# Gathered rows cover 256 output features instead of 128 in an expert layer on one core

## The reference, cut to what matters

```python
# z: 256 tokens x 2048, 8 heads, 128 x 128 experts, top 16 of each head
q = z @ peer_wq                               # queries
v1, i1 = top_k(q_first @ keys1, 16); v2, i2 = top_k(q_second @ keys2, 16)
top_s, expert = top_k(v1[i] + v2[j], 16)      # 16 experts of 16384 per head
gate = softmax(top_s)
act  = gelu(peer_u[expert] . z)
out  = sum over 8 heads and 16 picks of gate * act * peer_v[expert]
```

## Time and profile before

| | |
|---|---|
| median of three runs | 3079.88 us |
| the profiled execution, its own time | 3061.2 us |
| its span, first to last instruction | 3059.4 us |
| TensorE matmul busy | 3048.6 us (100%) |
| VectorE busy | 2092.8 us (68%) |
| ScalarE busy | 1562.2 us (51%) |
| GpSimd busy | 1022.9 us (33%) |
| HBM traffic over the span | 213 GB/s |

### The profile page before, as it was taken

The page is one execution under the profiler, slowest core; times in us unless marked ns, Lnnn a source line. Parts: engine busy times, 40 slices in busy tenths (PEclk is TensorE's granted clock), DMA queues, the critical chain, the costliest instruction groups (busy, mean ns, idle before and its releaser), DMA issues.

```text
span 3059.4 us, 42401 instructions
## 1 busy us (share of the span) xinstructions
PE 3048.6 (100%) x16292; PEld 2627.0 (86%) x16292; DVE 2092.8 (68%) x3013; ACT 1562.2 (51%) x2160; POOL 1022.9 (33%) x760
## 2 busy tenths in 40 slices
PE   9999999999999999999999999999999999999999
PEld 7888888888888888888888888888888888888887
DVE  8957985555555666566666789998766855545554
ACT  7654454444554444444444756666566534444443
POOL 0022368888860277666663300000432100000000
PEclk9999999999999999999999999999999999999999
DMA  6557877888876788888886655555555555566664
GB/s 255 172 202 263 319 216 195 240 214 215 213 215 213 255 256 267 264 264 266 268 242 202 193 184 175 173 176 189 188 191 175 190 169 210 188 205 194 194 194 148
DMA packets 388410, 653.91 MB, mean 214 GB/s; under 512 B 65008, under 2 KB 290544, under 8 KB 384752
## 3 DMA queue, kind: packets, MB, share of 16 engines
q1 hardware_dynamic: 306144, 574.70, 58.0%
q10 hardware_dynamic: 37008, 67.88, 6.3%
q0 software_dynamic: 45056, 8.62, 3.7%
HBM read 615.30 MB, written 35.79 MB: 213 GB/s over the span
## 4 chain that ended last, share of the span: by engine, by line
PE 94%; DVE 3%; DMA 1%; ACT 1%; issue 1%; POOL 0%; SPq 0%; ACTq 0%; DVEq 0%; POOLq 0%
PE G L536 40%; PE G L540 20%; PE G L591 4%; PE G L592 4%; PE G L593 4%; PE M L592 3%; PE M L593 3%; PE M L591 3%; PE M L618 2%; PE G L618 2%; PE M L620 2%; PE G L620 2%; PE M L619 2%; PE G L619 2%; DVE lo L1301 1%; DVE CV L1710 1%
## 5 line engine op out<-in xcount | busy, mean ns | idle before, releaser
L1301 DVE TENSOR_TENSOR lo<-raw,hi 128x1024 fp32r<-128x1024 f32 x1088 | 1381.0, 1284 | 567.6 <-ACT hi L918 565.2
L536 PE MATMUL G<-ZA,hi 128*128 128x512 f32 x5098 | 1765.0, 395 | 3.8 <-DVE lo L1301 2.3
L918 ACT ACTIVATE hi<-raw 128x1024 fp32r<-128x1024 f32 x1088 | 1127.4, 1055 | 606.6 <-DMA raw<-in_pv 342.7
L540 PE MATMUL G<-ZA,lo 128*128 128x256 f32 x5114 | 1389.2, 278 | 0.0
L536 PEld LDWEIGHTS G<-ZA,hi 128*128 128x128 f32 x5098 | 943.1, 188 | 210.1 <-DVE lo L1301 2.8
L540 PEld LDWEIGHTS G<-ZA,lo 128*128 128x128 f32 x5114 | 960.8, 188 | 16.6
L2009 POOL DMA_INDIRECT g_scratch<-sel,IDX x256 | 418.4, 1635 | 112.9 <-issue 81.5
L925 ACT ACTIVATE tA<-G 128x256 f32<-128x256 f32 x367 | 139.4, 380 | 578.4 <-PE G L540 577.9
L1307 DVE TENSOR_TENSOR tS<-G,tA 128x256 f32<-128x256 f32 x336 | 141.0, 420 | 326.7 <-ACT tA L925 323.5
L591 PE MATMUL G<-hi,ZB 128*128 128x512 f32 x512 | 199.5, 390 | 0.9 <-DVE lo L1301 0.9
L592 PE MATMUL G<-lo,ZB 128*128 128x512 f32 x512 | 199.2, 389 | 0.0
(11 more groups left out here) (373 smaller groups left out, 2818.6 us busy)
## 6 DMA issues: line engine op xcount, KB each, us to landing
raw<-in_pu SPq DMA_DIRECT2D x256, 512.0 KB, 4.4
raw<-in_pv SPq DMA_DIRECT2D x256, 512.0 KB, 5.2
raw<-in_w_in SPq DMA_DIRECT2D x192, 512.0 KB, 3.5
raw<-in_w_up SPq DMA_DIRECT2D x128, 512.0 KB, 3.5
raw<-in_w_down SPq DMA_DIRECT2D x128, 512.0 KB, 5.0
raw<-in_w_out SPq DMA_DIRECT2D x32, 512.0 KB, 3.5
raw<-in_wq SPq DMA_DIRECT2D x32, 512.0 KB, 4.4
g_scratch<-zero ACTq DMA_DIRECT2D x16, 1024.0 KB, 6.9
```

Of the source, the lines that this page charges most:

```text
L536: pe.matmul(G[:, 0:512], w, Z[:, k, :], start=first, stop=False, skip_group_check=True)
L540: m = pe.matmul(G[:, 0:256], lo[POS[u][p] % NRAW][:, k % 8, :], weights(u, p)[1][:, k, 0:256], start=False, stop=last, skip_group_check=True)
L918: act.activation(hi[w][:, :, :], raw[r][:, :].rearrange("p (k n) -> p k n", k=8), ACT.Copy).then_inc(s_hi, 1)
L1301: dve.tensor_tensor(lo[r][:, :, :], raw[r][:, :].rearrange("p (k n) -> p k n", k=8), hi[w][:, :, :].bitcast(F32), ALU.subtract).then_inc(s ...
```

## The change

- `EDGE` becomes 256: in the last quarter of each chunk the matmuls of the second 128 tokens have 256 columns instead of 384.
- The picked rows cover 256 features. Each pick needs two row DMAs of 128 features and one activation DMA: 384 indirect DMAs in all instead of 256. They come in 16 pieces of 8 picks (16 row DMAs and 8 activation DMAs), 16/5 for each unit. The dots of a piece begin three units after its last pick's unit, and are 256 wide. The ring has three pieces again.
- `load_g` and `load_h` become four DMAs of 512 KB each, two units apart: the gates of chunk c at `VB[c]` - 16, 14, 12, 10, the activations of chunk c at `VB[c-2]` + 8, 10, 12, 14. Each but the first waits until the one before has landed; a gate quarter also waits until GpSimd has used the same quarter of the chunk before. `gate_kept` waits for its own quarter instead of the whole.

```diff
-EDGE = 384
-PIECES = 8
+WIDE = 256
+EDGE = 512 - WIDE
+BLOCK = 8
+PIECES = 128 // BLOCK
+ROWS = WIDE // 128 * BLOCK
+RING = 3
 def picks_by(u):
-    return max(0, min(32 * PIECES, (u - VB[0] + 1) * 9 // 4))
+    return max(0, min((ROWS + BLOCK) * PIECES, (u - VB[0] + 1) * 16 // 5))
 for _b in range(PIECES):
-    _u = min(v for v in range(VB[0], F0) if picks_by(v) >= 32 * _b + 32) + 2
+    _u = min(v for v in range(VB[0], F0) if picks_by(v) >= (ROWS + BLOCK) * (_b + 1)) + 3
     _n = 4 if _b == PIECES - 1 else 2
-    for _k in range(0, 16, _n):
-        DOTS_AT.setdefault(_u + _k // _n, []).extend(range(16 * _b + _k, 16 * _b + _k + _n))
+    for _k in range(0, BLOCK, _n):
+        DOTS_AT.setdefault(_u + _k // _n, []).extend(range(BLOCK * _b + _k, BLOCK * _b + _k + _n))
+def slot_of(b):
+    return (b - PIECES) % RING
...
-                    [("vrow", [128, 3, 16, 128], F32), ("vacc", [128, 2, 128], F32)])
+                    [("vrow", [128, RING, BLOCK, WIDE], F32), ("vacc", [128, 2, WIDE], F32)])
...
-                if i in (0, 4, 8):
-                    act.wait_ge(s_dot, 96 + 4 * i)
+                if i % (12 // RING) == 0 and i < 12:
+                    act.wait_ge(s_dot, 128 - BLOCK * (RING - 1 - i * RING // 12))
...
+            def load_g(c, n):
+                size, k = 4 * 128 * T, slice(4 * n, 4 * n + 4)
+                at = size * (4 * c + n)
+                if c:
+                    act.wait_ge(s_gta, 4 * c - 4 + n + 1)
+                if c or n:
+                    act.wait_ge(s_gc, 64 * c + 16 * n)
+                src = scr[at:at + size, :].rearrange("(j i t) o -> i j (t o)", j=4, i=128)
+                act.dma_start(Gc[:, k, :], src).then_inc(s_gc, 16)
+            def load_h(c, n):
+                k = slice(4 * n, 4 * n + 4)
+                if n == 0:
+                    act.wait_ge(s_za, 8 * (c - 2) + 8)
+                    for m in range(4):
+                        act.wait_ge(s_hs[m], 64 * (c - 1))
+                if c >= 4 or n:
+                    act.wait_ge(s_hr[c % 2], 64 * (c // 2 - 1) + 16 * n)
+                act.dma_start(HB[c % 2][:, k, :].rearrange("p j t -> p (j t)"),
+                              hscr[c][:, 4 * n * T:4 * n * T + 4 * T]).then_inc(s_hr[c % 2], 16)
...
+                c, n = divmod(u - VB[0] + 16, 16)
+                if n in (0, 2, 4, 6) and c in range(KEPT):
+                    load_g(c, n // 2)
+                if n in (8, 10, 12, 14) and c - 1 in range(KEPT - 2):
+                    load_h(c + 1, (n - 8) // 2)
...
-                b = k // 16
-                if k % 16 == 0:
+                b = k // BLOCK
+                if k % BLOCK == 0:
...
-                    dve.wait_ge(s_hpk, 2048 + 256 * (b + 1))
+                    dve.wait_ge(s_hpk, 2048 + 16 * BLOCK * (b + 1))
...
-                    dve.wait_ge(s_vrow, 2048 + 256 * (b + 1))
+                    dve.wait_ge(s_vrow, 2048 + 16 * ROWS * (b + 1))
...
-                    pool.wait_ge(s_hr[c % 2], 16 * (c // 2))
-                pool.wait_ge(s_gc, 16 * c + 16)
+                    pool.wait_ge(s_hr[c % 2], 64 * (c // 2 - 1) + 16 * (n + 1))
+                pool.wait_ge(s_gc, 64 * c + 16 * (n + 1))
...
-                x, k = divmod(n, 16)
-                b = x // 2
-                if x % 2 == 0:
+                b, k = divmod(n, ROWS + BLOCK)
+                if k < ROWS:
...
-                            pool.wait_ge(s_vrow, 2048 + 256 * b)
-                        if b >= 3:
-                            pool.wait_ge(s_dot, 16 * (b - 2))
-                    pool.indirect_dma_start(vrow[:, (b + 1) % 3, k, :], None, pv_rows,
-                                            bass.IndirectOffsetOnAxis(IXV[:, 16 * b + k:16 * b + k + 1], 0)).then_inc(s_vrow, 16)
+                            pool.wait_ge(s_vrow, 2048 + 16 * ROWS * b)
+                        if b >= RING:
+                            pool.wait_ge(s_dot, BLOCK * (b - RING + 1))
+                    k, m = divmod(k, WIDE // 128)
+                    at = BLOCK * b + k
+                    pool.indirect_dma_start(vrow[:, slot_of(b), k, 128 * m:128 * m + 128], None, pv_rows,
+                                            bass.IndirectOffsetOnAxis(IXV[:, at:at + 1], 0),
+                                            element_offset=m * 16384 * 128).then_inc(s_vrow, 16)
```

More of the change, by code:

```diff
@@ L1235, in scalar_program @@
                         act.activation(sel[:, t, :], sel[:, t, :], ACT.Exp).then_inc(s_sfe, 1)
-                if u == VB[0] - 8:
+                if u == VB[0] - 16:
                     act.wait_ge(s_ind[0], 2048)
                     act.wait_ge(s_ind[1], 2048)
[L1239 to L1246, removed]
+                c, n = divmod(u - VB[0] + 16, 16)
[3 more added lines that the diff above has]
+                    load_h(c + 1, (n - 8) // 2)
                 if u == F0 + 2:
@@ L1597, in picked_index @@
                 dve.tensor_copy(whole, second).then_inc(s_ixa, 1)
-                dve.tensor_scalar(a, first, 8.0, 15.0 * 16384, ALU.mult, ALU.add).then_inc(s_ixa, 1)
+                dve.tensor_scalar(a, first, 8.0, float((16 - WIDE // 128) * 16384), ALU.mult, ALU.add).then_inc(s_ixa, 1)
                 dve.tensor_scalar(b, first, 4096.0, tcol[:, 1:2], ALU.mult, ALU.add).then_inc(s_ixa, 1)
@@ L1679, in expert_out @@
                 else:
-                    dve.wait_ge(s_dot, 16 * PIECES)
+                    dve.wait_ge(s_dot, 128)
                     dve.tensor_copy(by_token(q, 1)[:, 0:EDGE], VM[q][1][:, 0:EDGE])
@@ L2021, in pick @@
                         else:
-                            pool.wait_ge(s_vrow, 2048 + 256 * b)
-                        if b >= 3:
-                            pool.wait_ge(s_dot, 16 * (b - 2))
-                    pool.indirect_dma_start(vrow[:, (b + 1) % 3, k, :], None, pv_rows,
-                                            bass.IndirectOffsetOnAxis(IXV[:, 16 * b + k:16 * b + k + 1], 0)).then_inc(s_vrow, 16)
+                            pool.wait_ge(s_vrow, 2048 + 16 * ROWS * b)
[6 more added lines that the diff above has]
+                                            element_offset=m * 16384 * 128).then_inc(s_vrow, 16)
                 else:
-                    if k == 0 and b == 0:
+                    if k == ROWS and b == 0:
                         for n in range(4):
                             pool.wait_ge(s_hs[n], 64 * (KEPT - 2))
-                    elif k == 0:
-                        pool.wait_ge(s_hpk, 2048 + 256 * b)
-                    pool.indirect_dma_start(asp[:, 16 * b + k:16 * b + k + 1], None, hflat,
-                                            bass.IndirectOffsetOnAxis(IXA[:, 16 * b + k:16 * b + k + 1], 0)).then_inc(s_hpk, 16)
+                    elif k == ROWS:
+                        pool.wait_ge(s_hpk, 2048 + 16 * BLOCK * b)
+                    at = BLOCK * b + k - ROWS
+                    pool.indirect_dma_start(asp[:, at:at + 1], None, hflat,
+                                            bass.IndirectOffsetOnAxis(IXA[:, at:at + 1], 0)).then_inc(s_hpk, 16)
             pool.memset(zero[:, 0:512], 0.0).then_inc(s_pad, 1)
```

4 lines of the change are left out of this document (2 added, 2 removed).

## The result

The changed kernel took 3123.27 us, the median of 4 executions (3112.90 to 3129.94), against 3085.38 us for the kernel before (3067.36 to 3092.16). The ratio is 1.0129, 95% interval 1.0074 to 1.0184: slower, by 1.3%. The forecast was 3113 us, on a scale on which before was 3079.9 (a ratio of 1.0108). The profiled execution took 3112.9 us (span 3111.1); before it was 3061.2 (3059.4). The profiled pair is 51.7 us apart and the medians 38, so a sum made against the traces is some 14 us longer than what the medians show.

What follows compares the result with a forecast made beforehand. TensorE was taken to bound the kernel before, GpSimd the changed stage, hiding the 23 us spared. The stage ends 33 us later: 3061.2 + 33 = 3094 us profiled, 3113 us on the medians' scale; range 3060 to 3137.

Steps and rivals of the forecast that it cites:

- The main step: GpSimd in the changed stage: its reserve of 15 us a chunk is smaller than the 24 us of work added.
- What TensorE is spared: Last-quarter matmuls: 384 of them go from 384 to 256 columns, saving 23 us; a narrow unit takes 4.18 us.
- Where it shows: VectorE waits about 4 us before the small product once per 7.5 units from the third chunk; TensorE's gaps sum to some 55.
- The price of a pick: GpSimd's time per indirect DMA in the stage: 1.588 us each, the last pick starting near 1742 us.
- The third rival: Port between VectorE and GpSimd: wider dots hold up picks, at most 18 us more, +51 in all, 3131 us; chance 0.12.
- Landing: Time for a piece's last gather to arrive after its pick: taken as 4 us, since no row shows it.
- The clock: TensorE's granted clock could fall in its gaps, costing nothing while TensorE waits for GpSimd.
- The end of the stage: After the last picks, landing, VectorE's work and TensorE's last units end the stage at 1770.5 us, 33 us later than before.
- Edits at nothing: Quarter loads on ScalarE's queue: taken as 0, between bounds of -0.9 and +5 us; no stall at unit 168.
- The narrower matmuls as a rival: Last-quarter matmuls on TensorE are no cheaper when narrower; would change the sum by under 3 us; no chance stated.

Runs made afterwards that it cites:

- e1: The changed kernel with 128 picked features again (384 columns, 256 indirect DMAs), quarter loads, pieces and ring kept: 3061.41 us, ratio 0.9979 to the kernel before.
- e4: The changed kernel with one indirect DMA of 256 features per pick instead of two of 128: 3040.48 us, ratio 0.9897 to the kernel before.
- f3: The changed kernel with all 384 picks, its 32 gate products on VectorE instead of GpSimd: 3040.70 us, ratio 0.9932 to the kernel before.
- e2: The changed kernel with all picks, but TensorE's last-quarter matmuls back at 384 columns, the extra ones unused: 3104.88 us, ratio 1.0134 to the kernel before.
- e3: The changed kernel with all 384 picks, but dots only 128 features wide after the first two picks: 3103.48 us, ratio 1.0118 to the kernel before.
- f1: The one-DMA-per-pick version of the changed kernel, widened to 384 features, 128-column matmuls, pieces of 4: 3038.43 us, ratio 0.9932 to the kernel before.
- f2: The one-DMA-per-pick version of the changed kernel, widened to 512 features, that half block's matmuls left out: 3018.98 us, ratio 0.9860 to the kernel before.

## Why the prediction was right, point by point

- **The main step stands.** GpSimd has no reserve left: no waits for `Gc` in the whole stage, and it sets the end. e1, e4 and f3 take the load away in three ways and the time comes back; e2 shows that TensorE's own work no longer counts. How near the number came is in part luck: the sum had 33 us, the traces show 51.7 and the medians 38, of a kernel whose executions lie 17 to 25 us apart.
- **What TensorE is spared**: 23 us. Held: the group of six matmuls takes 1.05 us, a narrow unit so 4.18 as worked out, and f3's stage ends at 1715.3 for "about 1715".
- **Where it shows.** The first wait of VectorE in front of the small product ends at 1312 us, after 8.0 us, in the third to fourth chunk ("used up in the third chunk"); TensorE's first gap comes at 1361. Then VectorE waits at each of ten pieces in a row, for 6 to 14 us, 107.6 us in all, not for the 4 that was forecast. TensorE has gaps of 7 to 10 us at every other piece, two of 2 us between them, and 12.2, 4.9 and 1.9 us at the turns. Their sum is 56.7 us, for a forecast of "some 55": the sum was right, its parts were not.
- **The price of a pick** was set too low for this trace. From 1054.9 to the last end at 1756.2 are 701.3 us; less 28 x 2.42 for gate products (67.8) and 5.6 for six squares, 627.9 us for 384 picks: 1.635 us against 1.588 predicted, 18 us over the stage in this trace. The last pick was due at 1742 and came at 1755.2. In e2 and e3 it comes at 1742.1 and 1743.7, where the same sum gives 1.60 us a pick, inside the forecast's 1.55 to 1.63. So the price was nearly right, and most of the 13 us is one execution against another.
- **What lengthens a pick** is in the timelines of GpSimd and VectorE side by side:

```profile
1678.75 3.96 POOL L2042 DMA_INDIRECT vrow<-in_pv,IXV  x1 [0.30 <-issue]
1683.01 10.85 POOL L2042 DMA_INDIRECT vrow<-in_pv,IXV  x1 [0.30 <-issue]
1694.16 0.96 POOL L2042 DMA_INDIRECT vrow<-in_pv,IXV  x1 [0.30 <-issue]
```

```profile
1682.59 2.35 DVE L1317 TENSOR_TENSOR lo<-raw,hi 128x1024 fp32r<-128x1024 f32 x2
1684.86 1.28 DVE L1714 TENSOR_TENSOR ZB<-A,ZB 128x512 fp32r<-128x512 f32 x2
1686.07 2.35 DVE L1317 TENSOR_TENSOR lo<-raw,hi 128x1024 fp32r<-128x1024 f32 x2
1688.34 1.28 DVE L1714 TENSOR_TENSOR ZB<-A,ZB 128x512 fp32r<-128x512 f32 x2
1689.54 3.48 DVE L1317 TENSOR_TENSOR lo<-raw,hi 128x1024 fp32r<-128x1024 f32 x3
1694.47 1.23 DVE L1317 TENSOR_TENSOR lo<-raw,hi 128x1024 fp32r<-128x1024 f32 x1 [1.45 <-ACT hi L927]
```

One pick lasts 10.85 us. VectorE works without a pause until 1693.0, and the pick ends at 1693.9. In the whole stage nine picks of the changed kernel last over 3 us, 43.6 us in all, and each begins in such an unbroken run of VectorE; the kernel before has none longer than 2.50 us. These nine are 32 us more than nine picks at 1.29; the other 375 took 469.3 us, 1.25 each, 15 less. That is 17 of the 18 us. The timelines tie it down further, to one kind of instruction. Of the 136 picks over 1.3 us, 135 end 0.80 to 0.87 us after the end of a `lo` or a `ZB` operation (here 1693.02 and 1693.86), and none in the same way after a dot; of the 203 that took the shortest time, 1.0 us or less, 8 do. In the kernel before it is 103 of 104. It feeds itself: a late piece makes VectorE wait, then it catches up in one run (25.2 us long here), and that run holds up the next picks. That `lo` and `ZB` hold up picks rests on this agreement in time, found in e2, e3 and f3 too; no experiment isolates it, and the mechanism is open.
- **The third rival**, the port between VectorE and GpSimd, was put on the wrong instructions. Wider dots do nothing (e3). By the ends above it is the `lo` and `ZB` operations that hold up picks, singly by up to 1 us or so and in a run for longer. The Trainium skill, page "SBUF — State Buffer", section "Who interferes with whom", infers that descriptor generation is not held by a `tensor_tensor` with both inputs in SBUF, and the prediction named the rule without settling it; `lo` and `ZB` are such operations, and the 10.85 us and the 135 of 136 speak against that inference.
- **Landing** was taken as 4 us, for want of a row, and that was about right. In the ten pieces for which VectorE waited, the small product starts 1.6 to 5.2 us after the end of the piece's last pick, 3.6 on average (1713.84 to 1715.43 is the shortest).
- **The clock** was set at nothing because TensorE would be waiting. After the 9.83-us gap matmuls start 0.43 us apart, where 0.228 is usual: the granted clock from 1493 to 1497 us is 0.50, that is 1.2 GHz for 2.4, and the table has 0.88 to 0.96 from 1350 us on. Within a chunk TensorE is waiting anyway. At the end nobody waits for a later piece, and the slow matmuls after the last turns count. From the end of the last pick to the last matmul it took 31.9 us (1756.2 to 1788.1), where 27.8 was forecast (1742.7 to 1770.5).
- **The end of the stage** was forecast at 1770.5 and came at 1788.1 in this trace, at 1776.6 in e2 and 1775.2 in e3. Of the 17.6 us, 13.5 lie in the picks and 4 in the tail after them.
- **Edits at nothing** (quarter loads, ring, pieces of 8): e1 agrees. ScalarE's loads at unit 168 stall nothing: TensorE is busy 150.0 of the 150 us from 900 to 1050.
- **The narrower matmuls as a rival** ("no cheaper") fell here, but came true one step further on, in f1.

## What to carry to other kernels

Before giving an engine more of a kind of instruction, count the starts, not the bytes: a gather that is split in two costs the issuing engine twice, and one that moved twice the bytes cost it about the same (1229 against 1286 ns here). Compare that with its idle time per period in the stage concerned (here 15 us of reserve for 24 us of work), not with its busy share of the run. And where the gain goes to an engine that is full, first take other work off the engine that pays: the same picks with the gate products elsewhere, or with one DMA a row, turned 1.3% slower into 0.7 to 1.0% faster.

## What the hardware showed that I had not expected

- Indirect DMAs of 128 rows cost GpSimd 1.24 to 1.43 us at 512 bytes a row, 1.23 at 1 KB, 1.52 at 1.5 KB and 1.58 at 2 KB (means of e1, f3 and the change, e4, f1, f2), each with 0.3 us of issue before it. The shortest take 0.95 us at each of the four sizes, so the bytes set no part of that floor; the means of f1 and f2 hold seven and eight DMAs of more than 2.5 us, up to 9.3. With VectorE idle they start 1.26 us apart.
- One indirect DMA lasted 10.85 us beside a run of `lo` and `ZB` operations without a pause, and lengthened ones end 0.83 us or so after such an operation, in every trace of the series that was read for it (before, the change, e1, e2, e3, f3).
- 128-column matmuls in this pattern cost what 256-column ones do, 1.03 against 1.05 us for a group of six.
- A product of two 128x1024 float32 tiles takes 1.22 us on VectorE (f3) and 2.42 to 2.73 on GpSimd (the change and before).
- On one chip transfers, ScalarE, VectorE and TensorE's own issue came almost to a halt for tens of microseconds (47 GB/s, where the change has 280) while picks were issued without a break. What it takes for this, and whether the picks are its cause, is open.
